# Two blocks of a transformer, one core: q|k and g of the first block by seven of eight block products

## The chip, the cores and the metric

The kernel runs on 1 core of one Trainium2 chip. The metric is the device time of one execution in microseconds (us), lower is better. Time before: median 1560.25 us of 3 runs, 1560.14 to 1560.31.

## The reference

Two transformer blocks run on x of 512 tokens by 1024 features, all in float32. Only the start of the first block is touched:

```python
h = _rmsnorm(x, g_pre_mix)
proj = h @ w_in
q, k, v, g, u, sv, a_ret, a_sgu = jnp.split(proj, list(np.cumsum(IN_SPLITS)[:-1]), axis=-1)
y_ret = _retention_branch(q, k, v, g, ret_decay_logit, w_ret_o)
...
x = x + _rmsnorm(merged @ w_out, g_post_mix)
```

q and k are 512 columns each and are rotated (rope) before use; v and g are 1024 columns each. The retention multiplies q, k and v per head, and its normalized output is multiplied by silu(g).

## The kernel before

**How a float32 product is made.** Every float32 operand of the wide products is split into a rounded part (`hi`, fp32r) and a rest (`lo` = raw - hi), and each block product is three matmuls: hi by hi, hi by lo, lo by hi (`three`, lines 1006 to 1008). The normalized tokens are held transposed as `hT_hi` and `hT_lo`, eight blocks of 128 features by 512 tokens.

**Units.** The weights of w_in come in units of 2048 columns per partition (1 MB): four blocks of 128 features by 512 output columns. A unit is loaded by SyncE into one of two `raw` slots, its hi and lo parts go into one of two `w_hi`/`w_lo` slots, and TensorE runs 4 token tiles x 4 blocks x 3 = 48 matmuls over it (`unit_N`, line 1090). Two units (the two halves of the 1024 features) complete 512 output columns. In this phase GpSimd (POOL in the profile) makes both parts of nearly every unit (`split`, line 879: one `w_hi` over 2048, two `w_lo` over 1024 each). A unit of `GIVEN` gets its hi part from ScalarE instead (`give_hi`, line 1532).

**The phase.** The 12 units of `qkvg` are, in this order: q, k, v (2 x 512 columns), g (2 x 512 columns), two units each. `first_units` (line 1062) interleaves the first two with the transposes of h. Small transposes of two tables stand ahead of the fifth unit; the 32 transposes of the rotated q and k (`qk_T`) stand ahead of the last two. Each finished tile of 128 tokens by 512 columns lies in one of 8 PSUM banks until an engine has taken it: VectorE rotates the q and k tiles right out of PSUM (`rope`, line 2190, three operations per tile: lines 2200, 2201, 2208) and then computes the arguments of the decay table (lines 2220 to 2223); ScalarE copies v, applies silu to g, and copies the transposed q and k. Then come the retention (scores at line 1226, values at line 1238) and the units of sv, u and so on.

**What sets the order.** It is all written by hand: each engine runs its own list in order and waits on semaphores (`unit_split`, `unit_started`, `psum_ready`, `evacuated`). The buffers lie at fixed addresses; x occupies the first 16 KB of each partition and stays there until the residual sum after `out1`, far behind this phase.

**The scheme of seven products** exists already, in the first block's down projection (`set_product`, line 1280, 14 products, here called the set stage) and in the last MLP. A product of a 512-token matrix with 1024 x 1024 weights is cut in two along each of its three sizes, and seven block products replace eight. `PRODUCTS` names them: A11 B11, A12 B21, S1 T1, S2 T2, S4 B22, S3 T3, A22 T4, where A and B are quarters of the tokens and the weights and S and T sums of them. T1, T3 and T4 are made by DMAs that add into SBUF, issued by GpSimd (line 928); T2 by a VectorE addition (line 2396). One product is 2 token tiles x 4 blocks x 3 = 24 matmuls. Its results are added into up to three places: `CHAIN` says which PSUM banks a product adds onto, `TO_X` which rows and half take it.

## Time and profile before

| | |
|---|---|
| median of 3 runs | 1560.25 us |
| profiled execution, own time | 1559.91 us |
| its span | 1558.1 us |
| TensorE busy | 1539.6 us, 99% |
| VectorE / ScalarE / GpSimd busy | 953.1 / 553.2 / 729.9 us |
| granted TensorE clock | 0.998 of full speed |
| phase of q, k, v and g | from 9.5 to 149.5 us |
| retention | 149.5 to about 191 us |

The span is what the trace covers of the execution's own time; 1.8 us lie around it. PE is TensorE, PEld its weight loads, DVE is VectorE, ACT ScalarE, POOL GpSimd, SP SyncE. The phase is read from the first L1006 matmul to the first matmul of the scores (L1226).

### The profile page before, as it was taken

Reading aid. Unit: us, or ns where it says so; the run is one execution under the profiler, and the core shown is the slowest. Engines: PE = TensorE matmul, PEld = TensorE weight load, DVE = VectorE, ACT = ScalarE, POOL = GpSimd, SP = SyncE. Lnnn points to the kernel's source line nnn. Section 1 sums busy time; section 2 is a strip of 40 time slices with the busy share of each in tenths; the row PEclk is TensorE's granted clock in tenths of the full one; section 3 lists DMA queues with packets and bytes.
Section 4 is the critical chain, followed back from the end, with each engine's and each line's share of the span. In section 5 each row is a group of like instructions: output and inputs, shape, how many; then the busy total and the mean of one; then the engine's idle time right before and its main releaser. Section 6 shows DMA issues by size and latency. Waiting matters only on the chain.

```text
span 1558.1 us, 19118 instructions
## 1 busy us (share of the span) xinstructions
PE 1539.6 (99%) x7447; PEld 1268.1 (81%) x7447; DVE 953.1 (61%) x1226; ACT 553.2 (36%) x772; POOL 729.9 (47%) x295
## 2 busy tenths in 40 slices
PE   9999999999999999999999999999999999999997
PEld 6887788888888988888878897887778988888886
DVE  5901589830074554546884678997764336685878
ACT  3022211210124433334654435227643433334444
POOL 5875089687863244545553001431134263636451
PEclk9999999999999999999999999999999999999999
DMA  6242023143234133334674132231124164536362
GB/s 230 82 135 81 1 82 114 55 135 105 84 108 136 37 99 104 85 108 137 137 183 154 49 106 75 88 104 32 29 82 162 38 181 132 155 88 186 86 189 81
DMA packets 137686, 165.87 MB, mean 106 GB/s; under 512 B 5719, under 2 KB 98951, under 8 KB 137608
## 3 DMA queue, kind: packets, MB, share of 16 engines
q1 hardware_dynamic: 127478, 141.05, 28.2%
q0 software_dynamic: 8256, 18.88, 6.8%
q10 hardware_dynamic: 1874, 4.85, 1.0%
q8 instruction: 55, 0.90, 0.2%
q14 instruction: 23, 0.19, 0.0%
HBM read 156.37 MB, written 2.10 MB: 102 GB/s over the span
## 4 chain that ended last, share of the span: by engine, by line
PE 84%; POOL 5%; issue 5%; DVE 4%; ACT 2%; DMA 0%; POOLq 0%; DVEq 0%; ACTq 0%
PE ps L1006 25%; PE ps L1007 25%; PE ps L1008 25%; PE ps L1163 3%; PE ps L1238 2%; POOL w_lo L991 1%; PE ps L1436 1%; PE ps L1226 1%; POOL w_lo L989 1%; PE ps L1453 1%; POOL tail_lo L991 1%; POOL w_hi L891 1%; PE ps L1328 1%; DMA raw<-in_w_down 0%; POOL tail_lo L989 0%
## 5 line engine op out<-in xcount | busy, mean ns | idle before, releaser
L896 POOL TENSOR_TENSOR w_lo<-raw,w_hi 128x1024 fp32r<-128x1024 f32 x150 | 381.8, 2566 | 449.0 <-ACT w_hi L1539 446.3
L1006 PE MATMUL ps<-hT_hi,w_hi 128*128 128x512 f32 (+1 forms) x848 | 324.7, 383 | 1.0 <-POOL w_lo L896 0.5
L1007 PE MATMUL ps<-hT_lo,w_hi 128*128 128x512 f32 (+1 forms) x848 | 323.3, 381 | 0.0
L1008 PE MATMUL ps<-hT_hi,w_lo 128*128 128x512 f32 (+1 forms) x848 | 323.3, 381 | 0.0
L891 POOL TENSOR_TENSOR w_hi<-raw,cells 128x2048 fp32r<-128x2048 f32 x35 | 129.5, 3701 | 126.4 <-PE ps L1006 124.8
L1006 PEld LDWEIGHTS ps<-hT_hi,w_hi 128*128 128x128 f32 x848 | 159.4, 188 | 34.5 <-issue 2.3
L1008 PEld LDWEIGHTS ps<-hT_hi,w_lo 128*128 128x128 f32 x848 | 159.4, 188 | 30.9
L1007 PEld LDWEIGHTS ps<-hT_lo,w_hi 128*128 128x128 f32 x848 | 159.5, 188 | 30.0
L1006 PE MATMUL ps<-w_hi,hT_hi 128*128 128x512 f32 (+2 forms) x400 | 151.6, 379 | 0.5 <-POOL w_lo L915 0.5
L1007 PE MATMUL ps<-w_lo,hT_hi 128*128 128x512 f32 (+2 forms) x400 | 149.9, 375 | 0.0
L1008 PE MATMUL ps<-w_hi,hT_lo 128*128 128x512 f32 (+2 forms) x400 | 149.9, 375 | 0.0
L1539 ACT ACTIVATE w_hi<-raw 128x2048 fp32r<-128x2048 f32 (+1 forms) x50 | 94.3, 1886 | 66.9 <-PE ps L1006 48.3
L1006 PEld LDWEIGHTS ps<-w_hi,hT_hi 128*128 128x128 f32 x400 | 75.3, 188 | 14.1 <-POOL w_lo L915 0.9
L1008 PEld LDWEIGHTS ps<-w_hi,hT_lo 128*128 128x128 f32 x400 | 75.2, 188 | 13.3
L1007 PEld LDWEIGHTS ps<-w_lo,hT_hi 128*128 128x128 f32 x400 | 75.4, 189 | 12.6
L2359 DVE SCALAR_TENSOR_TENSOR taps<-ps,conv,taps 128x511 f32<-128x511 f32 x44 | 32.9, 748 | 83.4 <-ACT taps L1711 83.4
L1711 ACT ACTIVATE taps<-ps,conv 128x512 f32<-128x512 f32 x44 | 34.1, 777 | 125.7 <-PE ps L1008 125.7
L989 POOL TENSOR_TENSOR w_lo<-raw_tail,w_hi 128x1024 fp32r<-128x1024 f32 x13 | 34.9, 2686 | 82.7 <-ACT w_hi L1975 82.7
L2125 DVE TENSOR_TENSOR w_lo<-raw,w_hi 128x1024 fp32r<-128x1024 f32 (+1 forms) x20 | 22.0, 1144 | 65.0 <-ACT w_hi L1539 65.0
L1006 PE MATMUL ps<-w_hi,a_hi 128*128 128x512 f32 x152 | 59.4, 391 | 1.2 <-DVE w_lo L2711 0.6
L1008 PE MATMUL ps<-w_hi,a_lo 128*128 128x512 f32 x152 | 59.2, 389 | 0.0
L1007 PE MATMUL ps<-w_lo,a_hi 128*128 128x512 f32 x152 | 59.1, 389 | 0.0
(415 smaller groups left out, 3184.1 us busy)
## 6 DMA issues: line engine op xcount, KB each, us to landing
raw<-in_w_in SPq DMA_DIRECT2D x86, 512.0 KB, 4.5
raw<-in_w_up SPq DMA_DIRECT2D x54, 512.0 KB, 4.8
raw<-in_w_down SPq DMA_DIRECT2D x30, 512.0 KB, 6.7
raw_tail<-in_w_up SPq DMA_DIRECT2D x22, 512.0 KB, 4.8
raw<-in_w_out SPq DMA_DIRECT2D x16, 512.0 KB, 4.2
raw_tail<-in_w_down SPq DMA_DIRECT2D x16, 512.0 KB, 5.4
raw<-in_w_down POOLq DMA_DIRECT2D x12, 512.0 KB, 9.2
raw<-in_w_ret_o SPq DMA_DIRECT2D x8, 512.0 KB, 4.0
```

What stands on the lines that cost most here:

```text
L891: nc.gpsimd.tensor_tensor(hi[:, 0:n], raw[:, s, 0:n], zero.broadcast_to([P, n]), ALU.add).then_inc(unit_hi, 1)
L896: nc.gpsimd.tensor_tensor(lo[:, c], raw[:, s, c], hi[:, c].bitcast(f32), ALU.subtract).then_inc(unit_split, 1)
L989: nc.gpsimd.tensor_tensor(lo[:, 0:UNIT // 2], tail_raw_of(v)[:, 0:UNIT // 2], hi[:, 0:UNIT // 2].bitcast(f32), ALU.subtract)
L991: nc.gpsimd.tensor_tensor(lo[:, UNIT // 2:UNIT], tail_raw_of(v)[:, UNIT // 2:UNIT], hi[:, UNIT // 2:UNIT].bitcast(f32), ALU.subtract).then ...
L1006: first = nc.tensor.matmul(dst, a_hi, b_hi, start=start, stop=False, skip_group_check=onto)
L1007: nc.tensor.matmul(dst, a_hi, b_lo, start=False, stop=False, skip_group_check=onto)
L1008: return first, nc.tensor.matmul(dst, a_lo, b_hi, start=False, stop=stop, skip_group_check=onto)
L1163: last = nc.tensor.transpose(ps[:, BANK[t], n * width:n * width + width], src, ident[0:k, 0:k])
L1238: last = nc.tensor.matmul(ps[:, BANK[t], nn * 256:nn * 256 + 256], sT[:, h % 2, mb, n0:n0 + P], v[:, mb, h * RET_DV:(h + 1) * RET_DV], sta ...
L1539: nc.scalar.activation(slot_of(u)[0][:, 0:n], raw[:, s, 0:n], ACT.Copy).then_inc(hi_given, 1)
L1711: nc.scalar.activation(taps[:, j % 2, c, :], bank(t + c), ACT.Identity, bias=conv[:, 3, bass.ds(col, 1)], scale=conv[:, 1, bass.ds(col, 1) ...
L2359: V.scalar_tensor_tensor(tap[:, 1:S], ps[:, BANK[t + c], 0:S - 1], conv[:, 0, bass.ds(col, 1)], tap[:, 1:S], ALU.mult, ALU.add).then_inc(l ...
```

## The change

v is now made first, by four units. ScalarE copies it out of PSUM, and it also makes the hi part of the fourth unit. q|k (as one matrix of 1024 columns, set q=0) and g (set q=1) are each made by seven products, 14 in all, of 24 matmuls each; four units of 48 per matrix go. The token sums S1 to S4 are made once, by VectorE and ScalarE, while v's units run, and serve both sets. There are three raw slots and three hi/lo slots; the third ones lie in the first 16 KB, over x, and in `gain`. x is loaded a second time, behind the loads of sv. ScalarE makes all hi parts. VectorE makes the lo parts of the products 2 to 6 of each set, GpSimd those of products 0 and 1, and GpSimd issues the adding DMAs for T1, T3 and T4, now all three from HBM. A finished half product e (two per product, e = 2v and 2v+1) is copied by ScalarE where it comes first into its rows (products 0, 2, 3, 6) and added by VectorE otherwise (1, 4, 5). Rotation now works from SBUF, on `qk`, two rows at a time, at four places between the lo parts; the decay arguments stand at products 9 and 10, and the transposes `qk_T` ahead of the last product. `rope_t` and the two table buffers move to other addresses. Cut to its core:

```diff
-TICKETS = [("h1", 8), ("qkvg", 8), ("conv_cols", 1), ("spatial_T", 1), ("vg", 12), ("qk_T", 8), ("g_end", 4), ("ret", 24), ("sv", 8),
+TICKETS = [("h1", 8), ("v", 8), ("conv_cols", 1), ("spatial_T", 1), ("qk_T", 8), ("ret", 24), ("sv", 8),
...
-UNITS = [("qkvg", 12), ("sv", 4), ("u", 4), ("a_ret", 4), ("y_ret", 4), ("a_sgu", 4), ("y_sgu", 4),
+UNITS = [("v", 4), ("sv", 4), ("u", 4), ("a_ret", 4), ("y_ret", 4), ("a_sgu", 4), ("y_sgu", 4),
...
-GIVEN = [0, *range(U0["out1"], N_UNITS)]
+GIVEN = [0, 3, *range(U0["out1"], N_UNITS)]
...
+QK_G_N = 14
+QK_G_RAW = ({"X": 2, "Y": 0, "Z": 1}, {"X": 1, "Y": 0, "Z": 2})
+QK_G_LOADS = ("B11", "B21", "B22", "B12")
+QK_G_HELD = {"B11": "X", "T1": "X", "T2": "X", "T4": "X", "B21": "Y", "B12": "Y", "T3": "Y", "B22": "Z"}
+QK_G_BANK = ({"a": 2, "b": 0, "c": 4}, {"a": 0, "b": 6, "c": 4})
+QK_G_COPIED = (0, 2, 3, 6)
...
+    by_vector = [w % 7 in VECTOR_LOW + (4,) for w in range(QK_G_N)]
...
+        qk_g_raw2 = at("qk_g_raw2", [P, UNIT], 0)
+        qk_g_hi3 = at("qk_g_hi3", [P, UNIT], 96 * KB, f32r)
+        qk_g_lo3 = at("qk_g_lo3", [P, UNIT], 8 * KB, f32r)
+        first_s = {name: [at(f"first_{part}_{name}", [P, 4, S // 2], A + (48 + 8 * m + k) * KB, dt)
+                          for part, k, dt in (("s_hi", 0, f32r), ("s_lo", 4, f32r), ("s", 4, f32))]
+                   for m, name in enumerate(("S1", "S2", "S3", "S4"))}
...
-            with sp.Fori(1, 3) as i:
-                for b in range(2):
+            for q in range(2):
+                for name in QK_G_LOADS:
+                    if q == 0 and name == "B11":
+                        sp.wait_ge(h_made, 2 * NT)
+                    elif q == 0 and name == "B21":
+                        sp.wait_ge(unit_split, 2 * (u + 3))
+                    elif q == 0 and name == "B22":
+                        sp.wait_ge(unit_split, 2 * (u + 4))
+                    elif name == "B12":
+                        await_qk_g_low(sp, 7 * q + 1)
+                    elif name == "B11":
+                        await_qk_g_low(sp, 4)
+                        await_qk_g_sum(sp, 0, "T2")
+                    elif name == "B21":
+                        await_qk_g_low(sp, 5)
+                    else:
+                        await_qk_g_low(sp, 6)
+                    dst = qk_g_raw(q, name).rearrange("p (k n) -> p k n", k=4)
+                    src = qk_g_block(q, int(name[1]) - 1, int(name[2]) - 1)
                     for h in range(2):
-                        load(u + 2 * b + h, w1[:, h * 4:h * 4 + 4, bass.ds(i * 1024 + b * 512, 512)], 4, i, 4)
+                        sp.dma_start(dst[:, 2 * h:2 * h + 2, :], src[:, 2 * h:2 * h + 2, :]).then_inc(
+                            qk_g_loaded[qk_g_turn(q, name)[0]], 16)
+            await_qk_g_low(sp, QK_G_N - 2)
+            await_qk_g_low(sp, QK_G_N - 1)
             for b in range(2):
                 for h, src in enumerate(wide("w_in", IN1_SV + b * 512)):
                     load(U0["sv"] + 2 * b + h, src, 4)
+            sp.wait_ge(qk_g_ready, 2 * QK_G_N)
+            for t in range(NT):
+                sp.dma_start(x[:, t, :], a["x"][0, t * P:(t + 1) * P, :]).then_inc(x_again, 16)
...
-            split_all(2, U0["out1"])
+            split(2)
...
+            def qk_g_sum(q, name, addend):
+
+                out = qk_g_raw(q, name).rearrange("p (k n) -> p k n", k=4)
+                for h in range(2):
+                    half = slice(2 * h, 2 * h + 2)
+                    pool.dma_start(out[:, half, :], addend[:, half, :], accum_op=ALU.add).then_inc(qk_g_summed[name], 16)
+
+            for v in range(QK_G_N):
+                q, n = divmod(v, 7)
+                if n == 1:
+                    await_qk_g_low(pool, 7 * q)
+                    qk_g_sum(q, "T1", qk_g_block(q, 0, 1))
+                elif n == 2:
+                    await_qk_g_loaded(pool, q, "B12")
+                    qk_g_sum(q, "T3", qk_g_block(q, 1, 1))
+                elif n == 4:
+                    await_qk_g_low(pool, 7 * q + 3)
+                    qk_g_sum(q, "T4", qk_g_block(q, 1, 0))
+                if qk_g_low(v)[0]:
+                    continue
+                hi, lo = qk_g_slot(v)
+                pool.wait_ge(qk_g_hi, v + 1)
+                for half in range(2):
+                    c = slice(half * UNIT // 2, (half + 1) * UNIT // 2)
+                    made = nc.gpsimd.tensor_tensor(lo[:, c], qk_g_raw_of(v)[:, c], hi[:, c].bitcast(f32), ALU.subtract)
+                made.then_inc(qk_g_lows[0], 1)
+            pool.wait_ge(qk_g_ready, 2 * QK_G_N)
+            split_all(U0["sv"], U0["out1"])
...
-            first_units(T0["qkvg"])
-            for n in range(1, 6):
-                if n == 2:
-                    table_transposes()
-                if n == 5:
+            first_units(T0["v"])
+            for h in range(2):
+                unit_N(U0["v"] + 2 + h, T0["v"] + 4, 4, 512, 4 * h, h == 0, h == 1)
+            table_transposes()
+
+            def qk_g_product(v):
+
+                n = v % 7
+                hi, lo = [w.rearrange("p (k n) -> p k n", k=4) for w in qk_g_slot(v)]
+                name = PRODUCTS[n].split()[0]
+                l_hi, l_lo = first_tokens(name)
+                await_qk_g_low(pe, v)
+                if name[0] == "S":
+                    pe.wait_ge(first_s_lo, TOKEN_LOWS.index(name) + 1)
+                for t in range(2):
...
+                    if used:
+                        await_qk_g_taken(pe, used[-1])
+                    else:
+                        pe.wait_ge(evacuated[b], BANK[:T0["qk_T"]].count(b))
...
+            for at_v in range(QK_G_N):
+                if at_v == QK_G_N - 1:
+                    pe.wait_ge(qk_rotated, 2 * NT)
+                    for e in (12, 13, 16, 17, 22, 23):
+                        await_qk_g_taken(pe, e)
                     for tt in range(NT):
                         for w in range(2):
-                            pe.wait_ge(qk_rotated, 4 * w + tt + 1)
                             transposes(T0["qk_T"] + 2 * tt + w, [qk[:, w, tt, h * P:(h + 1) * P] for h in range(RET_H)])
-                for h in range(2):
-                    t = T0["qkvg"] + 4 if n == 1 else T0["vg"] + 4 * (n - 2) if n < 5 else T0["g_end"]
-                    unit_N(U0["qkvg"] + 2 * n + h, t, 4, 512, 4 * h, h == 0, h == 1)
+                qk_g_product(at_v)
...
-            decay_exp(0)
-            decay_exp(1)
...
+                nc.scalar.activation(qk_g_slot(v)[0], qk_g_raw_of(v), ACT.Copy).then_inc(qk_g_hi, 1)
+
+            def qk_g_copy(e):
+
+                if e // 2 % 7 in QK_G_COPIED:
+                    act.wait_ge(qk_g_ready, e + 1)
+                    row, half = qk_g_row(e)
+                    func = ACT.Silu if e >= 2 * QK_G_N - 2 else ACT.Copy
+                    nc.scalar.activation(row, ps[:, qk_g_bank(e), :], func, scale=-1.0 if half else 1.0).then_inc(
...
+            for tt in range(NT):
+                evacuate_v(0, tt)
+            give_hi(U0["v"] + 3, started=True)
+            qk_g_high(0)
+            for n, name in enumerate(TOKEN_SUMS):
+                act.wait_ge(first_s_made, n + 1)
+                nc.scalar.activation(first_s[name][0][:, :, :], first_s[name][2][:, :, :], ACT.Copy).then_inc(first_s_hi, 1)
+            qk_g_high(1)
+            for tt in range(NT):
+                evacuate_v(1, tt)
...
-            await_evacuated(act, T0["h1"] + 7)
+            for at_v in range(QK_G_N):
+                if at_v:
+                    qk_g_copy(2 * at_v - 1)
+                if at_v + 2 < QK_G_N:
+                    qk_g_high(at_v + 2)
+                if at_v == QK_G_N - 1:
+                    for tt in range(NT):
+                        for w, dst in ((0, qT), (1, kT)):
+                            t = T0["qk_T"] + 2 * tt + w
+                            evacuate(t, dst[:, :, tt * P:(tt + 1) * P], ACT.Copy,
+                                     bank(t).rearrange("p (h n) -> p h n", h=RET_H))
+                    silu_row(2 * at_v - 2)
+                    silu_row(2 * at_v - 1)
+                qk_g_copy(2 * at_v)
+                if at_v == 10:
+                    silu_row(16)
+                    silu_row(17)
+                elif at_v == 11:
+                    decay_exp(0)
+                    decay_exp(1)
+                elif at_v == 12:
+                    silu_row(22)
+                    silu_row(23)
+            qk_g_copy(2 * QK_G_N - 1)
...
-            for w in range(2):
-                for tt in range(NT):
-                    t = T0["qkvg"] + 4 * w + tt
-                    await_psum(dve, t)
-                    rope(bank(t), qk[:, w, tt, :], RET_H, RET_DK // 2, rope1, tt, rope_t, t, rotated["qk"])
...
+                if n not in QK_G_COPIED:
+                    row, half = qk_g_row(e)
+                    first = [w for w in range(e) if w // 14 == e // 14 and TO_X[w // 2 % 7] == TO_X[n] and w % 2 == e % 2]
+                    await_qk_g_taken(dve, first[-1])
+                    dve.wait_ge(qk_g_ready, e + 1)
+                    V.tensor_tensor(row, row, ps[:, qk_g_bank(e), :], ALU.subtract if half else ALU.add).then_inc(
+                        qk_g_added, 1)
...
+                out = qk_g_raw(q, "T2")
+                await_qk_g_loaded(dve, q, "B22")
+                await_qk_g_low(dve, 7 * q + 2)
+                V.tensor_tensor(out, out, qk_g_raw(q, "B22"), ALU.add).then_inc(qk_g_t2, 1)
...
+            def whole(out, name):
+
+                step.up(V.tensor_tensor(out, quarter(hT_hi, name).bitcast(f32), quarter(hT_lo, name).bitcast(f32), ALU.add))
...
+            for n in range(2 * NT):
+                await_evacuated(dve, T0["h1"] + n)
+            s1, s2, s3_, s4 = [first_s[name][2][:, :, :] for name in ("S1", "S2", "S3", "S4")]
+            whole(s2, "A11")
+            whole(s1, "A21")
+            whole(s4, "A22")
+            step.wait()
+            V.tensor_tensor(s3_, s2, s1, ALU.subtract).then_inc(first_s_made, 1)
+            V.tensor_tensor(s1, s4, s1, ALU.subtract).then_inc(first_s_made, 1)
+            dve.wait_ge(first_s_made, 2)
+            V.scalar_tensor_tensor(s2, s1, -1.0, s2, ALU.mult, ALU.subtract).then_inc(first_s_made, 1)
+            whole(s4, "A12")
+            step.wait()
+            dve.wait_ge(first_s_made, 3)
+            V.scalar_tensor_tensor(s4, s4, -1.0, s2, ALU.mult, ALU.subtract).then_inc(first_s_made, 1)
...
-            decay_args(0)
-            decay_args(1)
+            for at_v in range(QK_G_N):
+                q, n = divmod(at_v, 7)
+                if at_v:
+                    qk_g_take(2 * at_v - 1)
+                if n == 1:
+                    qk_g_weight_sum(q)
+                if at_v + 2 < QK_G_N and qk_g_low(at_v + 2)[0]:
+                    qk_g_weight_low(at_v + 2)
+                qk_g_take(2 * at_v)
+                for e in {2: (2, 3), 5: (8, 9), 6: (10, 11), 8: (12, 13)}.get(at_v, ()):
+                    rotate(e)
+                if at_v in (9, 10):
+                    if at_v == 9:
+                        dve.wait_ge(qk_rotated, 2 * NT)
+                    decay_args(at_v - 9)
...
+            dve.wait_ge(g_silu, 6)
+            await_qk_g_taken(dve, 2 * QK_G_N - 1)
...
+            dve.wait_ge(x_again, 16 * NT)
```

The helpers left out carry the counts of the semaphores: `qk_g_turn`, `qk_g_bank`, `qk_g_low`, `qk_g_taken`, the `await_...` functions, `quarter`, `first_tokens` and `qk_g_row`.

Where the order of instructions moves, by engine. On TensorE, around the transposes of q and k (`ident,qk`), before:

```order
L1007 MATMUL ps<-w_lo,hT_hi 128x512
L1008 MATMUL ps<-w_hi,hT_lo 128x512
L1163 MATMUL ps<-ident,qk 128x128 x32
L1006 MATMUL ps<-w_hi,hT_hi 128x512
L1007 MATMUL ps<-w_lo,hT_hi 128x512
```

and in the change:

```order
L1174 MATMUL ps<-qk_g_lo_93,first_s_hi_S_100 128x512
L1175 MATMUL ps<-qk_g_hi_92,first_s_lo_S_101 128x512
L1330 MATMUL ps<-ident,qk 128x128 x32
L1173 MATMUL ps<-w_hi,hT_hi 128x512
L1174 MATMUL ps<-w_lo,hT_hi 128x512
```

The 32 transposes had two units, 96 matmuls, behind them before the retention, and have one product, 24 matmuls, now. Over the whole program TensorE's list is 48 rows shorter.

On VectorE, from product 3 of the first set to the rotation at product 6 (L2478 is a lo part, L2464 the addition of a half product out of PSUM, L2446, L2447 and L2454 one rotation of a tile):

```order
L2478 TENSOR_TENSOR w_lo<-raw,w_hi 128x2048
L2478 TENSOR_TENSOR qk_g_lo_93<-qk_g_raw_91,qk_g_hi_92 128x2048
L2464 TENSOR_TENSOR qk<-qk,ps 128x512 x3
L2446 TENSOR_TENSOR rope_t<-qk,rope_107 128x512
L2447 TENSOR_TENSOR rope_t<-qk,rope_107 128x512
L2454 TENSOR_TENSOR qk<-rope_t 128x512
L2446 TENSOR_TENSOR rope_t<-qk,rope_107 128x512
L2447 TENSOR_TENSOR rope_t<-qk,rope_107 128x512
L2454 TENSOR_TENSOR qk<-rope_t 128x512
L2464 TENSOR_TENSOR qk<-qk,ps 128x512
```

The three additions are e = 8, 9 and 10; six operations of the rotation stand between them and the addition e = 11.

On GpSimd, from the fourth unit's lo parts to the second set's product 1 (L1082 is half a lo part, L1063 half an adding DMA):

```order
L1033 TENSOR_TENSOR w_lo<-raw,w_hi 128x1024 x4
L1082 TENSOR_TENSOR qk_g_lo_93<-qk_g_raw_91,qk_g_hi_92 128x1024 x2
L1063 DMA qk_g_raw_91<-in_w_in 128x2x512 x2
L1082 TENSOR_TENSOR w_lo<-raw,w_hi 128x1024 x2
L1063 DMA raw<-in_w_in 128x2x512 x2
L1063 DMA qk_g_raw_91<-in_w_in 128x2x512 x2
L1082 TENSOR_TENSOR w_lo<-raw,w_hi 128x1024 x2
L1063 DMA raw<-in_w_in 128x2x512 x2
L1082 TENSOR_TENSOR w_lo<-raw,w_hi 128x1024 x2
```

The units of before had a `w_hi` of 2048 and two `w_lo` each here; now GpSimd has four lo parts in 14 products, and its DMA issues stand between them.

## Rows read from the trace of the kernel before

**Rows 1.** The page: busy time of the engines.
```profile
PE 1539.6 (99%) x7447; PEld 1268.1 (81%) x7447; DVE 953.1 (61%) x1226; ACT 553.2 (36%) x772; POOL 729.9 (47%) x295
```
**Rows 2.** The page: the chain that ended last, by engine.
```profile
PE 84%; POOL 5%; issue 5%; DVE 4%; ACT 2%; DMA 0%; POOLq 0%; DVEq 0%; ACTq 0%
```
**Rows 3.** Windows: stretch, length, busy us of PE, PEld, DVE, ACT, POOL, clock, DMA.
```profile
59.00:150.00 91.00, 91.00 (x419) 75.70 (x418) 18.72 (x10) 16.67 (x29) 68.96 (x24) 1.00 0.33 106
```
**Rows 4.** Timeline of TensorE (start, duration): v's first unit, the first scores.
```profile
58.79 0.47 PE L1006 MATMUL ps<-w_hi,hT_hi 128*128 128x512 f32 x1
...
149.47 2.73 PE L1226 MATMUL ps<-qT,kT 128*128 128x512 f32 x6
```
**Rows 5.** Timeline of ScalarE: first and last v tile of four; transposed q and k.
```profile
94.47 0.60 ACT L1530 ACTIVATE v<-ps 128x512 f32<-128x512 f32 x1 [12.88 <-PE ps L1008]
...
102.63 0.60 ACT L1530 ACTIVATE v<-ps 128x512 f32<-128x512 f32 x1 [2.12 <-PE ps L1008]
...
124.89 0.59 ACT L1530 ACTIVATE qT<-ps 128x512 f32<-128x512 f32 x1
...
128.23 0.69 ACT L1530 ACTIVATE kT<-ps 128x512 f32<-128x512 f32 x1
```
**Rows 6.** Waits of TensorE in the set stage, 735 to 835 us.
```profile
PE ps L1006 <- POOL w_lo L954: 1.6, 2, 1.1
PE ps L1006 <- DVE w_lo L2430: 0.6, 1, 0.6
PE ps L1006 <- DVE h_added L2389: 0.2, 1, 0.2
```
**Rows 7.** Groups of the set stage, 752 to 825 us: busy us, mean ns.
```profile
L1757 ACT ACTIVATE set_a_hi<-f 128x1024 fp32r<-128x1024 f32 x11 | 11.5, 1056 | 13.6 <-PE ps L1006 13.6
L1743 ACT ACTIVATE w_hi<-raw 128x2048 fp32r<-128x2048 f32 x5 | 9.6, 1913 | 5.8 <-DVE raw L2396 5.8
...
L2389 DVE TENSOR_TENSOR h_added<-h_added,ps 128x512 f32<-128x512 f32 x17 | 10.9, 675 | 0.0
...
L2430 DVE TENSOR_TENSOR w_lo<-raw,w_hi 128x2048 fp32r<-128x2048 f32 x3 | 6.8, 2282 | 0.8 <-ACT w_hi L1743 0.8
...
L2396 DVE TENSOR_TENSOR raw<-raw 128x2048 f32<-128x2048 f32 x1 | 2.3, 2282 | 0.0
...
L2408 DVE TENSOR_TENSOR f<-f 128x1024 f32<-128x1024 f32 x1 | 1.2, 1208 | 0.0
```
**Rows 8.** Timeline of VectorE: end of the decay's rates; additions of the rope.
```profile
36.45 0.17 DVE L2184 TENSOR_SCALAR cells<-cells 128x8 f32<-128x8 f32 x1
...
42.20 1.38 DVE L2208 TENSOR_TENSOR qk<-rope_t 128x512 f32<-128x512 f32 x1
...
47.82 3.83 DVE L2208 TENSOR_TENSOR qk<-rope_t 128x512 f32<-128x512 f32 x1
...
58.70 0.69 DVE L2208 TENSOR_TENSOR qk<-rope_t 128x512 f32<-128x512 f32 x1
```
**Rows 9.** Timeline of GpSimd: one half lo part, one hi part, one lo part undisturbed.
```profile
42.99 2.85 POOL L896 TENSOR_TENSOR w_lo<-raw,w_hi 128x1024 fp32r<-128x1024 f32 x1
...
47.51 3.60 POOL L891 TENSOR_TENSOR w_hi<-raw,cells 128x2048 fp32r<-128x2048 f32 x1 [1.66 <-PE ps L1006]
...
84.82 4.73 POOL L896 TENSOR_TENSOR w_lo<-raw,w_hi 128x1024 fp32r<-128x1024 f32 x2
```
**Rows 10.** Timeline: an adding DMA of the set stage issued, its user on ScalarE.
```profile
788.12 2.46 POOL L928 DMA_DIRECT2D raw<-in_w_down  x2 [14.08 <-DVE w_lo L2430]
...
796.47 1.91 ACT L1743 ACTIVATE set_hi<-raw 128x2048 fp32r<-128x2048 f32 x1 [3.66 <-DMA raw<-in_w_down]
```
**Rows 11.** The page: DMA issues, count, KB each, median us to landing.
```profile
raw<-in_w_in SPq DMA_DIRECT2D x86, 512.0 KB, 4.5
...
raw<-in_w_down POOLq DMA_DIRECT2D x12, 512.0 KB, 9.2
```
**Rows 12.** Timeline of GpSimd: the hi part of sv's second unit.
```profile
191.30 3.60 POOL L891 TENSOR_TENSOR w_hi<-raw,cells 128x2048 fp32r<-128x2048 f32 x1 [43.82 <-PE ps L1006]
```

139 lines of the change are left out of this document (120 added, 19 removed).

## The prediction

> **What bounds the kernel now.** I read the page's busy times first, then the chain, then windows over the phase that is changed. The reader is to see one thing in all three: TensorE is the bound nearly everywhere. It is busy 99% of the span [rows 1], it carries 84% of the chain that ended last [rows 2], and between 59 and 150 us, where v, g and the transposes of q and k are made, it is busy 91.00 of 91 us at full granted clock, while VectorE has 18.7 and ScalarE 16.7 us of work and GpSimd 69.0 [rows 3]. So a matmul less in this phase is time gained, and every wait that the change opens on TensorE is time lost one for one, up to the next place where TensorE would have waited anyway; there is none in this stretch.
>
> **The matmuls.** Tiles of v end on TensorE every (102.63 - 94.47) / 3 = 2.72 us, and one is 12 matmuls, so a matmul costs 0.227 us [rows 5]. q, k and g have 8 units of 48 matmuls before, 384; now 14 products of 24, 336. 48 fewer make **-10.9 us**. The transposes are 32 in both.
>
> **A clock for the new part.** v's two first units take the places of q's, its two last those of k's, so product 0 starts where v's first unit starts now, at 58.8 us [rows 4], and product n at 58.8 + 5.44 n if nothing waits: 5 at 86.0, 6 at 91.4, 7 at 96.9. Call that start P(n). Durations: a hi part on ScalarE 1.9 us, a lo part or T2 on VectorE 2.3, an addition out of PSUM 0.7, an operation over 1024 columns 1.2 on VectorE and 1.06 on ScalarE [rows 7]; a lo part on GpSimd 4.7 undisturbed [rows 9]; a block made by an adding DMA, from issue to the start of its user, 796.47 - 788.12 = 8.35 us [rows 10].
>
> **How VectorE and GpSimd hinder each other.** This decides the largest loss. The addition that ends a rotation, both inputs in SBUF, takes 0.69 us at 58.70, when GpSimd rests, but 1.38 us from 42.20 and 3.83 us from 47.82 [rows 8]. GpSimd's half lo part before the one at 42.99 ends there, and 42.20 + 1.38 = 43.58, that is 0.59 behind it; the hi part from 47.51 ends at 51.11, and 47.82 + 3.83 = 51.65, 0.54 behind it [rows 9]. So the VectorE operation doesn't run at half speed: it stands until GpSimd's instruction is over, then runs at its own. The Trainium skill, SBUF — State Buffer, section "SBUF: two separate sides", states this as a rule: one shared port pair, an exclusive lock for a whole instruction, taken also by VectorE operations with two SBUF inputs. By that rule the trace agrees, and the sum below comes to 1553.9 us; read as half speed it would be 1552.0.
>
> **The bank that product 6 waits for.** In the first set, chain "a" lies in banks 2 and 3, and products 0, 3, 5 and 6 use it. The second half of product 6 may start at P(6) + 2.72 = 94.1 if e = 11, the second half of product 5, ready at 91.4, has been added by VectorE. Ahead of that addition stand e = 10 (ready 88.7, done 89.4) and six rotation operations. Before, two of three inputs of a rotation came from PSUM; now all are in SBUF. GpSimd starts the lo part of product 7 at 87.9 (hi part released by P(5), 1.9 us). Its first half ends at 90.3, so the first operation runs from 90.3, the second after it to 91.5; GpSimd's second half runs to 93.9; four operations of about 0.6 us with small gaps follow to 96.6; e = 11 is done at 97.3. TensorE waits 97.3 - 94.1 = 3.1 us. GpSimd issues T1's two DMAs from 93.9 for 2.46 us and then, at 96.3, starts the next lo part; if that catches the last operation, which starts at 96.0, another 2.4 us, 5.5 in all. With no hindrance at all the six operations end at 93.6 and the loss is 0. The two upper cases lie 0.3 us apart in time, so I take **+4.0 us**, between them; bounds 0 to 5.5.
>
> **Product 1.** VectorE starts the token sums at 36.6 [rows 8]: eight operations of 1.2 and up to three stands of 2.4 us behind GpSimd end by 53.5. ScalarE needs 1.06 and 1.9 us, at 56.5 product 1's hi part is there, and GpSimd's lo part, sharing with four lo parts of token sums (4.8 us), ends between 61.2 and 66.0; P(1) is 64.2. Bounds 0 to 1.8 us, I take **+0.5**, near the low end, since those four are done early.
>
> **The chain of sums in the second set.** T1 is issued behind GpSimd's lo part at 93.9, is used from 102.3, its hi part ends at 104.2, its lo part at 107.7 (VectorE rotates e = 10 and 11 to 105.4), T2 at 110.0, hi and lo part of product 10 at 114.2. P(10) with 4.5 us of delay is 117.7, so 3.5 us are left: **0**. The nearest case, the set stage, lost 2.4 us to waits of this kind over 14 products [rows 6]; bounds 0 to 2.4.
>
> **At nothing, with the cover.** VectorE, behind product 10's lo part, adds e = 16, rotates 12 and 13, adds 17 and makes product 11's lo part by about 122.1; P(11) is 123.1. This cover is one microsecond, and beyond it each microsecond counts. The copies of transposed q and k take 128.23 + 0.69 - 124.89 = 4.0 us on ScalarE [rows 5]; product 13 covers them with 5.4, where two units did with 21.8. The split of sv's first unit moves behind all products, 3.6 + 4.7 us under a retention of 40. Its second unit still waits for TensorE, as at 191.30 [rows 12]. The second load of x, four pieces of 512 KB at 4.5 us each or less on SyncE's queue [rows 11], goes out behind sv's last unit at about 185 and is needed behind `out1`, more than 20 units later; the unit of u queued behind it has one unit's time, 10.9 us, to arrive. Without that cover it would cost up to 7 us once. Silu in two steps and the tables that ScalarE reloads stand in its idle time.
>
> **The sum.** -10.9 + 4.0 + 0.5 + 0 = -6.4 us. From the profiled execution's 1559.9 that makes 1553.5; the median of the runs is 0.3 above that execution, so **1553.9 us**.
>
> **The rivals.**
> - *Hardly a wait.* GpSimd's lo part of product 7 comes earlier or later than I place it, the six operations go through at 0.7 us, and the losses stay under 2.5 us: 1549.4 to 1551.9. For it: of the three rope additions shown one isn't held up at all and one by only 0.7 us [rows 8], and a shift of a microsecond or two can move the operations out of GpSimd's way. Against it: GpSimd's start and VectorE's hang on the same P(5).
> - *The waits add up.* All terms at their upper bounds, 5.5 + 1.8 + 2.4 = 9.7 us: up to 1559.1. For it: the set stage shows that such chains do slip [rows 6], and here one set follows the other with three raw slots, not four.
> - *Slower: the adding DMAs set the pace.* All of T1, T2 and T4 of the second set pass through one raw slot. From the hi part of product 7 at P(5) to P(13) there are 8 x 5.44 = 43.5 us, and the chain takes 4.7 (GpSimd's lo part) + 4 x 1.9 (hi parts) + 4 x 2.3 (three lo parts and T2) = 21.5 us and two adding DMAs, T1 and T4. They fit up to 11.0 us each. For slower than before by over 0.2% the losses must exceed 14 us, 9.5 more than my 4.5, so each DMA has to take about 16 us. The trace shows 8.35 here [rows 10] and a median of 9.2 for a single piece in the last MLP [rows 11]. At 18 us each they lose 2 x 7.0 = 14.0 us beyond the 4.5, and the time is 1567.8. A rule of the Trainium skill points this way (SBUF — State Buffer, the same section): GpSimd writes the descriptors of its DMAs through that same port pair, and VectorE can starve it. In the one pair shown the issue took 2.46 us [rows 10], which is no sign of it; its chance is within this rival's.
>
> **How the numbers follow.** 0.2% of this time is 3.1 us, about what a measurement tells from no change: faster is below 1557.1, slower above 1563.4. My forecast, losses of 2.5 to 7 us, 1551.9 to 1556.4, has a chance of 0.52; hardly a wait 0.25; the waits add up, 1556.4 to 1559.1, 0.17, of which 0.08 still count as faster and 0.09 as the same; slower or nearly so 0.06, of which 0.05 is slower. Faster 0.85, the same 0.10, slower 0.05. The range runs from no loss at all, 1549.3, to 1557.5, which leaves out some 0.15.
>
> **What would show it.** 5843 rows of TensorE's list against 5891, the scores starting near 143.1 instead of 149.5 us. One wait of TensorE of 3 to 5.5 us in the second half of product 6, released by a VectorE addition out of PSUM; VectorE operations of the rotation near 90 us that last 1.4 to 3 us and end 0.6 behind a GpSimd instruction. At most small waits for lo parts elsewhere. Wrong would be: no wait at product 6 (first rival), several waits for lo parts from VectorE behind T1 and T2 (second), ScalarE idle for an adding DMA for more than 5 us in both sets (third), or a wait behind 150 us that the trace of before doesn't have, since all later work is to be only moved.

## The result

The changed kernel takes 1563.99 us (median of 14 runs, 1562.97 to 1564.95), the one before, run beside it, 1560.33 (14 runs). The ratio is 1.0022, 95% interval 1.0014 to 1.0029: **slower by 3.7 us**, where 6.4 us faster was forecast. The profiled execution took 1562.97 us with a span of 1561.0, against 1559.91 before, so its own difference is 3.06 us. Three runs behind this document took far longer, 2570 us (one of the sixth experiment) and 2589 and 3996 us (the kernel before); the medians hardly feel them (1557.1 for 1557.2 without the first), and no reading rests on them.

The page of the changed kernel, its busy times and its chain, against [rows 1, 2]:

```profile
PE 1531.2 (98%) x7399; PEld 1260.4 (81%) x7399; DVE 1005.7 (64%) x1262; ACT 595.0 (38%) x807; POOL 694.0 (44%) x290
...
PE 80%; POOL 6%; issue 5%; DVE 5%; ACT 2%; DMA 1%; POOLq 0%; DVEq 0%; SPq 0%; ACTq 0%
```

The 48 matmuls are gone (7399 for 7447), and TensorE is busy 8.4 us less; the span is longer all the same. Windows say where (columns as in [rows 3]):

```profile
59.00:150.00 91.00, 80.16 (x361) 66.03 (x361) 67.34 (x55) 45.63 (x50) 27.58 (x16) 0.94 0.59 141
150.00:192.00 42.00, 42.00 (x164) 30.87 (x163) 27.04 (x50) 7.94 (x12) 8.63 (x3) 1.00 0.16 51
```

In the changed stretch TensorE rests 10.8 us, where it rested not at all, and its mean granted clock is 0.94 for 1.00. The waits of TensorE from 0 to 190 us (total, times, longest) put all of it in one place; the two others of that answer (1.6 and 0.5 us) lie at 2 and 13 us, and the trace of before has them too:

```profile
PE ps L1173 <- DVE qk L2464: 10.8, 2, 10.1
```

L2464 is `qk_g_take`, VectorE's addition of a product's half out of PSUM. "Row e" here and below is the row that half product e goes into (e = 2v and 2v + 1, so rows 10 and 11 belong to product 5). The place is the forecast one: product 6's first half waits for the addition of row 10 (0.78 us), its second half for that of row 11 (10.06 us). What VectorE did before the second of them, by its timeline, against the rope additions of [rows 8]:

```profile
88.33 2.29 DVE L2478 TENSOR_TENSOR qk_g_lo<-qk_g_raw,qk_g_hi 128x2048 fp32r<-128x2048 f32 x1 [5.61 <-ACT qk_g_hi L1836]
90.54 1.87 DVE L2464 TENSOR_TENSOR qk<-qk,ps 128x512 f32<-128x512 f32 x3
92.33 1.08 DVE L2446 TENSOR_TENSOR rope_t<-qk,rope 128x512 f32<-128x512 f32 x1
93.33 2.89 DVE L2447 TENSOR_TENSOR rope_t<-qk,rope 128x512 f32<-128x512 f32 x1
96.26 0.69 DVE L2454 TENSOR_TENSOR qk<-rope_t 128x512 f32<-128x512 f32 x1
97.05 6.58 DVE L2446 TENSOR_TENSOR rope_t<-qk,rope 128x512 f32<-128x512 f32 x1
...
104.87 0.68 DVE L2464 TENSOR_TENSOR qk<-qk,ps 128x512 f32<-128x512 f32 x1
```

and GpSimd beside it, against [rows 9]:

```profile
90.19 5.48 POOL L1082 TENSOR_TENSOR w_lo<-raw,w_hi 128x1024 fp32r<-128x1024 f32 x2 [14.39 <-ACT w_hi L1836]
95.97 2.44 POOL L1063 DMA_DIRECT2D raw<-in_w_in  x2 [0.30 <-POOL w_lo L1082]
97.47 5.60 POOL L1082 TENSOR_TENSOR w_lo<-raw,w_hi 128x1024 fp32r<-128x1024 f32 x2
```

Two things stand in these rows. The lo part of product 7 (from 90.19) held two VectorE operations, one for each half: 1.08 and 2.89 us instead of 0.68. The lo part of product 8 (from 97.47, behind T1's DMA issues) held **one operation through both halves**: it stood from 97.05 until 0.56 us behind GpSimd's end at 103.07. And the whole sequence starts late: product 6's lo part at 88.33 had waited 5.61 us for its hi part, and that for T4, by ScalarE's timeline:

```profile
86.38 1.92 ACT L1836 ACTIVATE qk_g_hi<-qk_g_raw 128x2048 fp32r<-128x2048 f32 x1 [4.84 <-DMA qk_g_raw<-in_w_in]
```

T4, the block of weight sums that product 6 uses, was issued at 73.36, 13.0 us earlier; [rows 10] gave 8.35. The last part of the loss is the clock. Windows around the wait:

```profile
95.00:105.00 10.00, 0.54 (x3) 0.12 (x1) 9.83 (x6) 0.65 (x2) 7.77 (x5) 0.73 0.74 120
105.00:107.00 2.00, 1.39 (x3) 1.16 (x4) 1.97 (x4) 0.00 (x0) 0.00 (x0) 0.50 0.98 357
107.00:109.00 2.00, 2.00 (x6) 1.56 (x5) 1.86 (x4) 0.00 (x0) 0.16 (x1) 0.50 0.29 110
109.00:111.00 2.00, 2.00 (x8) 1.59 (x8) 0.61 (x1) 0.39 (x1) 2.00 (x2) 0.79 0.10 11
111.00:115.00 4.00, 4.00 (x20) 3.30 (x19) 1.96 (x1) 2.61 (x3) 0.28 (x1) 1.00 1.01 172
```

While TensorE rested, the granted clock fell to 0.50, its 1.2 GHz level, and stayed there until 109.6, 4 us into the work again: in TensorE's timeline matmuls take 0.63 us each up to 109.19, 0.40 from 109.95. TensorE's timeline at the wait's end and at product 7's start:

```profile
105.61 0.80 PE L1173 MATMUL ps<-qk_g_hi,hT_hi 128*128 128x512 f32 x1 [10.06 <-DVE qk L2464]
...
110.41 0.40 PE L1173 MATMUL ps<-w_hi,hT_hi 128*128 128x512 f32 x1
```

The second half of product 6 took 110.41 - 105.61 = 4.80 us instead of 12 x 0.227 = 2.72: 2.1 us. So -10.9 (the matmuls) + 0.8 + 10.1 (the two waits) + 2.1 (the clock) = +2.1. The scores start at 152.02 us against 149.47 [rows 4], +2.55; of the 0.4 between, product 6 was 0.3 late before its first wait (91.78 against 58.85 + 6 x 5.44). To the last matmul (1553.61 against 1550.75) 0.3 is added, a wait of 0.4 us at 502 us, for a row of h, that the trace of before doesn't have.

### The profile page after: what moved, and what is told of

It is laid out like the page before. It is cut to its first block, busy times and chain, and to the rows that moved or that the text cites. A ratio compares the mean times of both kernels' runs of the same rounds, so it can differ in the third digit from the quotient of the medians.

```text
span 1561.0 us, 19071 instructions
## 1 busy us (share of the span) xinstructions
PE 1531.2 (98%) x7399; PEld 1260.4 (81%) x7399; DVE 1005.7 (64%) x1262; ACT 595.0 (38%) x807; POOL 694.0 (44%) x290
## 4 chain that ended last, share of the span: by engine, by line
PE 80%; POOL 6%; issue 5%; DVE 5%; ACT 2%; DMA 1%; POOLq 0%; DVEq 0%; SPq 0%; ACTq 0%
PE ps L1173 24%; PE ps L1175 24%; PE ps L1174 24%; PE ps L1330 3%; PE ps L1433 2%; POOL w_lo L1033 1%; POOL w_lo L1158 1%; PE ps L1631 1%; PE ps L1421 1%; POOL w_hi L1028 1%; POOL w_lo L1156 1%; PE ps L1648 1%; POOL tail_lo L1158 1%; PE ps L1523 1%; DVE rope_t L2446 0%
## 5 line engine op out<-in xcount | busy, mean ns | idle before, releaser
L1033 POOL TENSOR_TENSOR w_lo<-raw,w_hi 128x1024 fp32r<-128x1024 f32 x134 | 342.0, 2573 | 454.3 <-ACT w_hi L1734 452.3
L1028 POOL TENSOR_TENSOR w_hi<-raw,cells 128x2048 fp32r<-128x2048 f32 x26 | 96.7, 3719 | 116.9 <-PE ps L1173 87.9
L1173 PE MATMUL ps<-w_hi,hT_hi 128*128 128x512 f32 (+2 forms) x304 | 114.2, 376 | 0.5 <-POOL w_lo L1052 0.5
L1174 PE MATMUL ps<-w_lo,hT_hi 128*128 128x512 f32 (+2 forms) x304 | 112.8, 371 | 0.0
L1175 PE MATMUL ps<-w_hi,hT_lo 128*128 128x512 f32 (+2 forms) x304 | 112.6, 370 | 0.0
L1173 PEld LDWEIGHTS ps<-w_hi,hT_hi 128*128 128x128 f32 x304 | 57.3, 189 | 10.4 <-POOL w_lo L1052 0.9
L1175 PEld LDWEIGHTS ps<-w_hi,hT_lo 128*128 128x128 f32 x304 | 57.4, 189 | 9.5
L1174 PEld LDWEIGHTS ps<-w_lo,hT_hi 128*128 128x128 f32 x304 | 57.4, 189 | 8.9
L2978 DVE TENSOR_TENSOR x<-x,ps 128x512 f32<-128x512 f32 x56 | 38.3, 683 | 33.6 <-PE ps L1175 33.1
```

The lines of the kernel that those rows point to most:

```text
L1028: nc.gpsimd.tensor_tensor(hi[:, 0:n], raw[:, s, 0:n], zero.broadcast_to([P, n]), ALU.add).then_inc(unit_hi, 1)
L1033: nc.gpsimd.tensor_tensor(lo[:, c], raw[:, s, c], hi[:, c].bitcast(f32), ALU.subtract).then_inc(unit_split, 1)
L1173: first = nc.tensor.matmul(dst, a_hi, b_hi, start=start, stop=False, skip_group_check=onto)
L1174: nc.tensor.matmul(dst, a_hi, b_lo, start=False, stop=False, skip_group_check=onto)
L1175: return first, nc.tensor.matmul(dst, a_lo, b_hi, start=False, stop=stop, skip_group_check=onto)
L2978: V.tensor_tensor(row, row, ps[:, TAIL_BANK[e], :], ALU.subtract if half else ALU.add).then_inc(tail_taken, 1)
```

## The experiments

All medians stand beside runs of the kernel before on the same chip (1560.37 to 1560.55 us), each from 5 to 11 runs; "the changed kernel" is 1563.99. In parentheses is the 95% interval of the ratio to the kernel before. The waits are those of one profiled execution of each version, and that one can lie up to 1.7 us from the median. **The hold** below is GpSimd holding a VectorE operation that has two inputs in SBUF.

**Rotations moved back.** The most direct test that VectorE's list is the place.

```diff
-                for e in {2: (2, 3), 5: (8, 9), 6: (10, 11), 8: (12, 13)}.get(at_v, ()):
+                for e in {2: (2, 3), 6: (8, 9), 7: (10, 11), 8: (12, 13)}.get(at_v, ()):
```

> The rotations of rows 8 and 9 of q move behind the addition of row 11, and those of 10 and 11 one product further back, behind product 9's lo part. Theory (VectorE's rotations, held by GpSimd, stand ahead of the addition that TensorE waits for): the 10.1 us wait in the second half of product 6 falls under 1.5 us, and with it the fall of the granted clock; what can be late next is product 9, whose lo part then stands behind two rotations and behind T1's adding DMA: a wait of 1 to 4 us there. 1550.5 to 1555 us. Rival (the chain of sums in raw slot X is late by itself, T4 and then T1, and the bank only shows it first): the wait goes to products 8 to 10 nearly whole, and the time stays above 1559 us.

Measured: 1559.33 us, ratio 0.9992 (0.9983 to 1.0001). The wait for row 11 is gone, one of 1.1 us for row 10 is left, and a new one of 4.4 us has come, at product 10 and not at product 9: there T2 stood behind the rotations of rows 10 and 11. Behind it the clock fell as before. So the theory holds for the 10 us, and the guess at what is late next was one product off. The time doesn't follow it: 1550.5 to 1555 us were expected, and 1559.33 lies where the rival had it, since of 10.8 us of waits 5.5 are still there, with the clock behind them. The rival's late chain isn't in it: ScalarE began T1's hi part at 104.64, and product 9 didn't wait.

**GpSimd's lo part of product 8 waits.** The rotations stay where they were; one lo part is taken out of VectorE's way.

```diff
+                if v == 8:
+                    await_qk_g_taken(pool, 11)
                 pool.wait_ge(qk_g_hi, v + 1)
```

> GpSimd's lo part of product 8 waits until row 11 has been added; nothing else is changed, the rotations of 8 and 9 stay ahead of that addition. Theory (one rotation operation was held through both halves of that lo part): the operation that lasted 6.58 us now ends some 0.6 us behind GpSimd's DMA issue, near 99.0 us, and lasts 1.9 us; the wait falls from 10.1 to about 5.4 us, and half of what the clock took comes back: 5 to 6 us less than the changed kernel, 1558 to 1559.5 us. If the DMA issue holds nothing, the operation lasts 0.7 and the wait is 4.2 us. Rival (the length of VectorE's list is the cause and the holding only apparent, or another instruction of GpSimd takes the place): the wait stays at 8 us or more and the time within 2 us of 1564.

Measured: 1558.77 us, 0.9988 (0.9979 to 0.9997), 5.2 less than the changed kernel; the wait is 4.16 us. VectorE's timeline, with GpSimd's DMA issues from 96.65 to 99.09 and the lo part from 100.45:

```profile
96.94 0.69 DVE L2456 TENSOR_TENSOR qk<-rope_t 128x512 f32<-128x512 f32 x1
97.74 0.69 DVE L2448 TENSOR_TENSOR rope_t<-qk,rope 128x512 f32<-128x512 f32 x1
98.35 0.69 DVE L2449 TENSOR_TENSOR rope_t<-qk,rope 128x512 f32<-128x512 f32 x1
99.07 0.69 DVE L2456 TENSOR_TENSOR qk<-rope_t 128x512 f32<-128x512 f32 x1
99.68 0.68 DVE L2466 TENSOR_TENSOR qk<-qk,ps 128x512 f32<-128x512 f32 x1
```

The operations beside the issues run at 0.69 us: a DMA issue on GpSimd holds nothing here. It was the two halves. They come later here, behind a wait of GpSimd's of 1.35 us, and now hold one operation each:

```profile
100.45 5.52 POOL L1084 TENSOR_TENSOR w_lo<-raw,w_hi 128x1024 fp32r<-128x1024 f32 x2 [1.35 <-DVE qk L2466]
```

```profile
100.88 2.87 DVE L2449 TENSOR_TENSOR rope_t<-qk,rope 128x512 f32<-128x512 f32 x1
103.78 2.74 DVE L2456 TENSOR_TENSOR qk<-rope_t 128x512 f32<-128x512 f32 x1
```

**Matmuls in the wait.** 40 matmuls from product 6's own operands into a free bank, so that TensorE doesn't rest.

```diff
+                    if v == 6 and t == 1:
+                        pe.wait_ge(evacuated[6], BANK[:T0["qk_T"]].count(6))
+                        for n_idle in range(40):
+                            nc.tensor.matmul(ps[:, 6, :], l_hi[:, n_idle % 4, 0:P], hi[:, n_idle % 4, :],
+                                             start=True, stop=True)
```

> 40 matmuls into a free bank, 9.1 us at full clock, stand in TensorE's list ahead of the wait of product 6's second half; they compute nothing that is used. The wait ends with the addition of row 11 as before. Theory (the granted clock fell because TensorE rested, and the 24 matmuls and what follows took 2.1 us more for it): the granted clock stays at 1.00, product 6's second half takes 2.7 instead of 4.8 us, and the time is about 2 us under the changed kernel's, 1562. Rival (the clock fell for another reason, or its cost stands beside other waits): no change, 1564; or, if the matmuls come out longer than the wait, a little more.

Measured: 1562.43 us, 1.0013 (1.0004 to 1.0022), 1.6 less than the changed kernel. The stretches that stood at 0.73 and 0.50 stand at 1.00:

```profile
95.00:105.00 10.00, 9.64 (x43) 7.66 (x41) 9.83 (x5) 0.65 (x2) 7.91 (x5) 1.00 0.73 117
105.00:107.00 2.00, 1.25 (x5) 1.05 (x6) 1.97 (x5) 0.00 (x0) 0.00 (x0) 1.00 0.96 347
```

The row is added as late as before (TensorE goes on at 105.75), but its half is done 1.8 us sooner (ScalarE's copy of it starts at 108.84 for 110.61). So the clock fell because TensorE rested: the wait is as long as before, and only what TensorE did in it has changed.

**x a third time.**

```diff
-            for t in range(NT):
-                sp.dma_start(x[:, t, :], a["x"][0, t * P:(t + 1) * P, :]).then_inc(x_again, 16)
+            for again in range(2):
+                if again:
+                    sp.wait_ge(x_again, 16 * NT)
+                for t in range(NT):
+                    sp.dma_start(x[:, t, :], a["x"][0, t * P:(t + 1) * P, :]).then_inc(x_again, 16)
...
-            dve.wait_ge(x_again, 16 * NT)
+            dve.wait_ge(x_again, 32 * NT)
```

> x is loaded a third time, behind the second, on the same queue: the cost of the second load of x is doubled, if it has one. Theory (it is covered): no change against the changed kernel, within 0.5 us of 1564, and no new wait of TensorE between 190 and 240 us. Rival (the second load delays u's first units and what is behind them on SyncE's queue, or is what is left of the loss): 1 to 7 us more, 1565 to 1571.

Measured: 1564.35 us, 1.0025 (1.0015 to 1.0036), 0.4 above the changed kernel, inside both intervals, and no wait of TensorE between 190 and 260 us. So the second load is covered.

**Rotations still further back.** `{2: (2, 3), 6: (8, 9), 8: (10, 11), 9: (12, 13)}` in the line of the first experiment.

> As the run with the rotations moved back, but one product further: rows 8 and 9 behind the addition of row 11, 10 and 11 behind product 10's lo part, 12 and 13 behind product 11's. There the wait had gone to product 10 (4.4 us), behind T2, which VectorE made only after rotating rows 10 and 11; now T2 follows the lo part of product 9 at once. Theory (the place of the rotations in VectorE's list is the whole of the loss): waits of 1.1 us at product 6 and under 1.5 us at product 10, no fall of the granted clock, 1551 to 1553.5 us, about 11 under the changed kernel and 7 to 9 under the one before. Rival (T1's adding DMA and the chain behind it are late by themselves): 3 us or more of wait at product 9 or 10, the clock falls, 1557 us or more.

Measured: 1558.79 us, 0.9991 (0.9982 to 1.0000), where 1551 to 1553.5 were expected: a miss. (The profiled execution took 1557.13.) The two waits at the forecast places are small (0.7 and 0.5), but new ones stand behind them:

```profile
PE ps L1173 <- DVE qk_g_lo L2478: 2.9, 1, 2.9
PE ps L1173 <- DVE w_lo L2478: 2.2, 2, 1.7
```

They are products 12 and 11. Both lo parts had their hi parts long since (product 12's was ready at 118.7, VectorE took it up at 128.93) and stood behind rotations and the decay's arguments. Neither theory nor rival had that: it was again the order of VectorE's list, further down. The clock didn't fall in the profiled execution.

**GpSimd's halves apart from its DMA issues.** Nothing else moves.

```diff
                 pool.wait_ge(qk_g_hi, v + 1)
+                if v == 8:
+                    nc.gpsimd.tensor_tensor(lo[:, 0:1], qk_g_raw_of(v)[:, 0:1], hi[:, 0:1].bitcast(f32),
+                                            ALU.subtract).then_inc(issue_over, 1)
+                    pool.wait_ge(issue_over, 1)
                 for half in range(2):
```

> The changed kernel, with one addition in GpSimd's list: behind T1's two DMA issues it makes the first column of product 8's lo part alone and waits for that, and only then makes the two halves; nothing else moves. In the changed kernel's trace the two halves behind the DMA issue overlap each other by 1.0 us in the records, and the VectorE operation stood through both; two halves with no issue ahead of them overlap by 0.04 us, and VectorE got in between them. Theory A (work that is queued behind a DMA issue runs as one piece, and only then shuts VectorE out for both halves): the operation that stood 6.58 us stands 2.5 to 3.5 us, VectorE gets in between the halves, and the addition of row 11 comes 2 to 4 us earlier; 1560 to 1562.5 us. Theory B (VectorE's operation, once waiting, always stands through what GpSimd has in its list, whatever was ahead): no change, 1564 us.

Measured: 1557.24 us, 0.998 (0.9971 to 0.9989), 6.7 less than the changed kernel for one column of work and GpSimd's own wait for it. The profiled execution took 1558.49, 4.5 less than that of the changed kernel, which is about what its waits lost (10.8 to 6.0); the rest of the 6.7 no trace shows. GpSimd and, below, VectorE:

```profile
97.04 2.44 POOL L1064 DMA_DIRECT2D raw<-in_w_in  x2 [0.30 <-POOL w_lo L1087]
98.54 1.64 POOL L1082 TENSOR_TENSOR w_lo<-raw,w_hi 128x1 fp32r<-128x1 f32 x1
100.25 5.14 POOL L1087 TENSOR_TENSOR w_lo<-raw,w_hi 128x1024 fp32r<-128x1024 f32 x2
```

```profile
98.12 0.69 DVE L2451 TENSOR_TENSOR rope_t<-qk,rope 128x512 f32<-128x512 f32 x1
...
100.06 0.68 DVE L2469 TENSOR_TENSOR qk<-qk,ps 128x512 f32<-128x512 f32 x1
100.66 2.50 DVE L2451 TENSOR_TENSOR rope_t<-qk,rope 128x512 f32<-128x512 f32 x1
103.08 2.85 DVE L2452 TENSOR_TENSOR rope_t<-qk,rope 128x512 f32<-128x512 f32 x1
```

Of the two theories A stands: behind the issues, the column and the two halves let VectorE in between (2.50, then 2.85, one operation for each half). The column isn't what matters: in the second experiment a wait of GpSimd's alone stood between the issues and the halves, with the same result (2.87 and 2.74). In every version without anything between them one operation stood through both halves, 6.58 to 6.89 us. Nor is it enough that GpSimd's halves are queued without a wait. Early in the changed kernel four stand one behind the other with no issue ahead, and three VectorE operations of 1.2 us there stand through one half each:

```profile
38.91 6.04 POOL L1033 TENSOR_TENSOR w_lo<-raw,w_hi 128x1024 fp32r<-128x1024 f32 x2 [5.55 <-ACT w_hi L1734]
44.90 6.73 POOL L1082 TENSOR_TENSOR qk_g_lo<-qk_g_raw,qk_g_hi 128x1024 fp32r<-128x1024 f32 x2
```

```profile
42.72 3.30 DVE L2497 TENSOR_TENSOR first_s_S<-first_s_S,first_s_S 128x1024 f32<-128x1024 f32 x1
45.95 3.41 DVE L2498 TENSOR_TENSOR first_s_S<-first_s_S,first_s_S 128x1024 f32<-128x1024 f32 x1
49.40 3.31 DVE L2500 SCALAR_TENSOR_TENSOR first_s_S<-first_s_S,first_s_S 128x1024 f32<-128x1024 f32 x1
```

So a DMA issue straight ahead of the halves is what the long stands have in common, and what the short ones here lack. More came back than expected, since row 11's addition slipped in just before the halves. The wait for row 11 is 4.17 us, nearly the 4.0 that the prediction had for it. That is in part luck: 4.0 stood between 3.1 without a catch by product 8's lo part and 5.5 with one, and here that lo part catches nothing ahead of row 11. Row 10's wait is 1.9 in this execution.

**B11 later.** On top of the fifth experiment, `await_qk_g_sum(sp, 0, "T4")` ahead of SyncE's load of the second set's B11.

> As the version with the rotations one product further back, and SyncE's load of block B11 of the second set waits until T4 of the first set has landed. T4 took 13.0 us from issue to its user in the changed kernel, against 8.8 of T1. Theory (T4 shares the DMA engines with that load and with B21's): T4 lands 2 to 4 us earlier, the 1.1 us wait in the first half of product 6 goes, B11 comes about as much later and its hi part stays behind that of product 6 anyway: 0 to 1.5 us less than without this edit. Rival (T4 is slow by itself, B11 becomes the late one): T1 of the second set is issued 2 to 3 us later and product 9 waits for it: 1 to 4 us more.

Measured: 1560.24 us, 1.0000 (0.9991 to 1.0009), 1.5 above the run without it, with intervals that overlap. T4's hi part starts at 83.93 instead of 86.42, so T4's adding DMA is slowed by that load, 10.7 us for 13.0, and product 6 waits no more. But B11's hi part comes at 89.39 instead of 88.25, product 8 waits 1.6 us for GpSimd's lo part, and products 10 to 12 wait as long as before or longer (0.9, 1.7 and 3.0 us for 0.5, 1.7 and 2.9). The clock fell behind the last of them, which it hadn't without the edit. The theory was right on the cause, and the time came out on the rival's side, for another product than its own (8, not 9).

**Matmuls in a short wait.** The second experiment, with 16 of the useless matmuls ahead of its wait of 4.2 us.

> As the run in which GpSimd's lo part of product 8 waits (a wait of 4.2 us at product 6, behind which the granted clock stood at 0.50 for some 6 us), with 16 matmuls of no use, 3.6 us, ahead of TensorE's wait. Theory (a rest of 4.2 us costs as much clock as one of 10): the granted clock stays at 1.00 and the time falls by 2 to 3 us against that run, to 1556 to 1557 us. Rival (the clock costs little here): within 1 us of it.

Measured: 1555.41 us, 0.9967 (0.9955 to 0.9980), 3.4 less than without them, a little more than the 2 to 3 expected. Windows of the second experiment's trace, and below of this one's:

```profile
96.00:100.00 4.00, 0.25 (x2) 0.00 (x0) 3.83 (x6) 0.60 (x1) 2.80 (x3) 0.93 0.32 36
100.00:102.00 2.00, 1.59 (x4) 1.30 (x5) 2.00 (x3) 0.00 (x0) 1.55 (x1) 0.50 1.10 198
...
104.00:106.00 2.00, 2.00 (x6) 1.62 (x5) 2.00 (x1) 0.06 (x1) 1.97 (x1) 0.50 0.32 57
```

```profile
96.00:100.00 4.00, 4.00 (x20) 3.29 (x19) 3.83 (x5) 1.00 (x2) 3.46 (x3) 1.00 0.33 66
```

A rest of 4.2 us cost TensorE as much clock as one of 10, or more: half speed until 106 us, where the matmuls keep it at 1.00.

**The edits together.** (a) Rotations spread, and GpSimd's column; (b) the spread alone; (c) GpSimd's column and the 16 matmuls, nothing else. The spread:

```diff
                     qk_g_weight_sum(q)
+                    if q:
+                        rotate(10)
...
+                for e in {2: (2, 3), 6: (8, 9), 8: (11,), 9: (12,), 10: (13,)}.get(at_v, ()):
...
+                if at_v in (10, 11):
+                    if at_v == 10:
+                        dve.wait_ge(qk_rotated, 2 * NT)
+                    decay_args(at_v - 10)
```

> Two edits together: VectorE's rotations are spread so that none stands ahead of something that TensorE waits for (rows 8 and 9 behind the addition of row 11, 10 between T2 and product 10's lo part, 11, 12 and 13 one to a product behind it, the arguments of the decay one product later), and GpSimd makes one column of product 8's lo part alone behind T1's DMA issues before the two halves. In the version with the rotations last, 2.95 and 1.70 us of its waits stood behind rotations and the decay's arguments. Theory: left are some 1 to 2 us at product 6's first half (T4's adding DMA) and under 1 us elsewhere, the granted clock doesn't fall: 1551.5 to 1554 us. Rival (the adding DMAs T3 and T4 of the second set are what products 12 and 13 wait for): those two waits stay, 1556 us or more.

Measured (a): 1557.43 us, 0.998 (0.9971 to 0.9989). The waits at products 10 to 12 are gone, so they weren't the DMAs'. But 3.1 us have come at the transposes, for row 23's addition, which the moved arguments of the decay now preceded; the clock fell to 0.52 behind it. The expectation of 1551.5 to 1554 missed this, and the time lies where the rival had it, for another reason.

> The same spread of the rotations, without the edit in GpSimd's list. Theory: a VectorE operation again stands 6 to 7 us through both halves, near 97 us, but nothing that TensorE waits for is behind it until product 9's lo part, which waits for T1's DMA anyway: within 1 us of the version with both edits. Rival (the hold still costs): 2 us or more above it.

Measured (b): 1557.16 us, the same interval, and the same 3.1 us at the transposes; a VectorE operation stood 6.89 us from 96.28, and no wait stands behind it before one of 0.8 at product 10. As expected: the hold costs what stands behind it, nothing by itself.

> The smallest mend of the change: only GpSimd's one column behind T1's DMA issues, and 16 matmuls of no use (3.6 us) ahead of TensorE's wait at product 6. Theory (the two losses, the long stand of VectorE and the fall of the clock, add up and each can be taken away by itself): 2 to 3 us less than with GpSimd's edit alone (1557.2 us), 1554.2 to 1555.2 us, granted clock 1.00 throughout.

Measured (c): 1555.45 us, 0.9967 (0.9955 to 0.9980), 1.8 less than with the column alone, a little short of the 2 to 3 expected (1554.2 to 1555.2): the two losses come off one by one.

**The decay's second arguments later still.** (a), with these arguments behind row 23.

```diff
                     qk_g_take(2 * at_v - 1)
+                if at_v == 12:
+                    decay_args(1)
```

> The version with both edits, and the decay's second set of arguments behind the addition of row 23 instead of ahead of it, with ScalarE's two exponentials one product later. In the version with both edits the only wait over 1.5 us was of 3.1 us, at the transposes of q and k, for row 23's addition behind those arguments, and the granted clock fell behind it. Theory (a rest and its clock are all that is left there): that wait goes with its clock, 4 to 5 us less, 1552 to 1554 us, and the runs lie closer together than the 4.5 us of that version, since no rest over 2 us is left for the clock to fall behind. Rival (the scores wait for the copies of transposed q and k, which the exponentials now hold up): a new wait of 2 us or more at the first scores, 1555 us or more.

Measured: **1554.86 us** (5 runs), 0.9965 (0.9951 to 0.9978): 2.6 less than (a), with intervals that overlap, 9.1 less than the changed kernel and 5.7 less than the kernel before, though above the 1552 to 1554 expected. It is the lowest median, but not to be told from the 1555.4 of the two versions with 16 matmuls. Its waits from 0 to 190 us, without that at the start and three of 0.5 or less:

```profile
PE ps L1178 <- DVE qk L2468: 1.4, 1, 1.4
PE ps L1335 <- ACT qT L1730: 1.2, 1, 1.2
PE ps L1335 <- DVE silu_g L2468: 0.8, 1, 0.8
```

The rival's cause is there, but not at its place nor with its 2 us: `L1335` are the transposes themselves. The last eight waited 1.2 us, from 135.95 to 137.19, for ScalarE's first copy out of a bank, which stood behind the two exponentials (134.86 to 136.65); the scores waited for nothing. The runs didn't come closer together (1553.18 to 1558.39), with no rest above 1.6 us in the profiled one; what sets that spread stays open.

## Why the prediction was wrong

**The matmuls**: right, 48 fewer. Product 0 started at 58.85 us for 58.8, and product 6 could have at 91.78 for 91.4.

**The bank that product 6 waits for**: the step that failed. Place, releaser and the kind of mechanism were right, the size was 10.8 us instead of 4.0 (bound 5.5), 10.1 of it at the forecast half. Two sentences in it were wrong. "Another 2.4 us, 5.5 in all" took it that one VectorE operation can be caught by one half at most, as in the three rope additions of [rows 8]. It was caught by two at once, 6.58 us; with that alone removed the wait was 4.2 us. The trace of before had such stands, outside the stretches that were read: 9.13 us twice, through halves of lo parts queued behind four DMA issues, and 7.10 us twice, through two halves behind two issues. VectorE's timeline at the first, and GpSimd's beside it:

```profile
1358.05 9.13 DVE L2692 SCALAR_TENSOR_TENSOR f<-f 128x1024 f32<-128x1024 f32 x1
```

```profile
1353.15 3.45 POOL L972 DMA_DIRECT2D raw_tail<-in_w_down  x2
1354.63 4.39 POOL L989 TENSOR_TENSOR w_lo<-raw,w_hi 128x1024 fp32r<-128x1024 f32 x1
1356.99 4.40 POOL L991 TENSOR_TENSOR w_lo<-raw,w_hi 128x1024 fp32r<-128x1024 f32 x1
1360.68 3.05 POOL L989 TENSOR_TENSOR tail_lo<-raw_tail,tail_hi 128x1024 fp32r<-128x1024 f32 x1
1363.04 3.05 POOL L991 TENSOR_TENSOR tail_lo<-raw_tail,tail_hi 128x1024 fp32r<-128x1024 f32 x1
```

An operation of 1.2 us stands 9.13, until 1.09 us behind the end of the last of four halves queued behind DMA issues. Later in the same stage GpSimd waited 1.25 us between such issues and two halves, and there VectorE was let in after the first (an operation from 1511.61 took 1.72 us, the next 3.42). So a stand through several halves could be read there before the change was run. Secondly, GpSimd's lo part of product 7 was placed at 87.9 by P(5) alone; it began at 90.19, since its hi part stood behind that of product 6, which waited for T4. The adding DMA of T4 in the first set had no term at all, and took 13.0 us where the DMAs of the sum were given 8.35. Row 10's addition ended at 92.41 instead of 89.4 us.

**The clock** had no term. The 1.00 of [rows 3] was taken for the changed kernel too, though it was measured where TensorE doesn't rest. Even the forecast wait of 4.0 us would hardly have gone without it: both experiments with waits of 4.2 us, the second and the sixth, show 0.50 behind them. Taken away by matmuls it gave back 1.6 us (wait of 10), 3.4 and 1.8 us (waits of 4.2). With 10.8 + 2.1 in place of 4.0, none for product 1, and the two slips of 0.3 and 0.4 us, the forecast's own sum gives 1559.9 - 10.9 + 12.9 + 0.7 = 1562.6 us, where the profiled execution took 1562.97.

**Product 1**: no wait, 0.5 allowed. **The chain of sums in the second set**: no wait in the changed kernel, as forecast, but that was no cover of its own: the 12 us lost at product 6 gave it its time. With them gone, products 10 to 12 waited up to 4.4 us in the first and fifth experiments, for VectorE's order, and 0.8 at most once that was mended. **At nothing**: the second load of x, the copies of q and k, silu, sv's split: right, but for 0.4 us at 502 us.

**The rivals.** "Hardly a wait" and "the adding DMAs set the pace" didn't happen: in the first set T1 took 8.8 us from issue to user (51.95 to 60.77), T4 13.0, under the 16 that this rival needed of each in the second, and no product of the second set waited. (The 9.2 us that the prediction took from [rows 11] for the last MLP is a median over both stages: 4 pieces of the set stage at 6.6 and 8 of the last MLP at 10.5.) "The waits add up" named the right kind of slip; its bounds were those of the single terms, and the one beyond its bound decided. The rule of the Trainium skill, SBUF — State Buffer, section "SBUF: two separate sides", speaks of a lock for a whole instruction: by that rule 4.0 us came out and the trace agrees as long as no DMA issue is ahead; behind one the VectorE operation stood through two instructions. The starving of descriptors, of the same section, no run here shows: T1's two issues took 2.44 us beside VectorE's work.

## What to carry over

When work moves to an engine that was idle, write out its list in order up to each thing that TensorE waits for; the 10.1 us here, and the waits of 4.4, 2.9, 1.7 and 3.1 us in the versions that came after, were each an addition, a sum or a lo part standing behind rotations or decay arguments that nobody needed yet. Where VectorE reads two SBUF inputs and GpSimd has plain work queued straight behind DMA issues, take the longest such stand in the trace as the bound, not the usual one, or put a small awaited instruction between, or a wait that has to stand there anyway. And price a wait of TensorE like these with the clock behind it: what the useless matmuls gave back, in waits of 4 and 10 us, was 1.6 to 3.4 us beyond their length.

## What was not expected of the hardware

Behind DMA issues, the records of GpSimd's two halves overlap by 1.0 us (97.47 to 100.78 and 99.77 to 103.07) where otherwise by 0.04, and one VectorE operation stands through both; with a wait of GpSimd's between, it is let in after each instruction. Why, the traces don't say; that spans of GpSimd in a profile are unreliable is a caution of the Trainium skill, Perfetto Trace Analysis, in its part on GpSimd's instructions, and the 1.0 us may be such. VectorE's lengths (6.58 us and 2.50) and the 6.7 us between the medians don't rest on those spans.

The granted clock fell behind the rests of 4.2, 4.4 and 10.1 us, and behind none of 2.1 or less. Of four rests of about 3 us it fell behind two (3.14 in (a), 2.96 with B11 later) and not behind the two others (3.11 in (b), 2.95 in the fifth experiment). The runs of those four versions lie 3.4 to 5.1 us apart, and this toss is only part of it. In (a) and (b) the slowest run, 4.5 and 4.7 us above the fastest, has a mean granted clock of 0.995 for the fastest's 0.999; over some 1554 us that difference is worth an estimated 6 us at most, so there the clock can be all of it. In the fifth experiment the slowest and the fastest run both have 0.998, and what lengthens the one by 5.1 us stays open. The Trainium skill, TensorE: Matmul & The Clock Gate, section on the HAM clock gate, has these two levels and ties them to how busy TensorE has been lately; the trace agrees, with 1.00 before and 0.50 behind the wait of product 6.
